# Split value-token projections, a row-paired decay and rate product, and branch gates moved into the delta rule's groups

## What is computed

```python
u = rmsnorm(h, g_mix[l])
proj = u @ w_in[l]
(rq, rk, rv, rgate, dq, dk_, dv_, dz, db, da, gate_r, gate_d) = split(proj)
ro = retention_chunkwise(rotary(rq), rotary(rk) * RET_DK ** -0.5, rv)      # 8 heads, values of 128
y_ret = (silu(rgate) * groupnorm(ro)) @ w_ret_br[l]
g = -exp(dn_a_log[l]) * softplus(da + dn_dt_bias[l])                       # summed along the tokens of a chunk
do = gated_delta_chunkwise(cq, ck, cv, g, beta)                            # 8 heads, (I + A)^-1 per chunk
y_dn = (norm(do) * silu(dz)) @ w_dn_br[l]
merged = sigmoid(gate_r) * y_ret + sigmoid(gate_d) * y_dn
h = h + merged @ w_o[l]                                                    # then a convolutional FFN
```

```python
w = -softplus(-(w0 + tanh(w_lo) @ w2)) - 0.5      # decay, w_lo is 64 wide, w2 is 64 x 2048
a = sigmoid(a0 + a_lo @ a2)                       # rate,  a_lo is 64 wide, a2 is 64 x 2048
decay = exp(-exp(w))
y = wkv7_scan(r, decay, k, v, -kk, kk * a)        # 32 heads of 64, worked two heads (a pair) at a time
```

## Time and profile before

| What | Value |
|---|---|
| Time, median of 3 runs | 1546.98 us (1546.9 to 1548.11) |
| Profiled execution's own time | 1548.26 us |
| Its span in the trace | 1546.5 us |
| PE busy | 1492.3 us, 96% |
| DVE, ACT, POOL busy | 1004.3, 861.8, 49.0 us |
| Chain that ended last | PE 88%, ACT 5%, DVE 4%, issue 2%, DMA 1% |
| HBM | 107 GB/s over the span |

### The profile page before, as it was taken

How to read it: one execution, slowest core, us unless ns; L and a number is a source line. 1 busy time by engine, 2 the same in 40 slices (tenths; PEclk the granted TensorE clock), 3 DMA queues, 4 the chain that set the end, 5 groups by cost and what they waited for, 6 DMA issues and landing times.

```text
span 1546.5 us, 27065 instructions
## 1 busy us (share of the span) xinstructions
PE 1492.3 (96%) x10620; PEld 1323.7 (86%) x10620; DVE 1004.3 (65%) x1907; ACT 861.8 (56%) x2071; POOL 49.0 (3%) x28
## 2 busy tenths in 40 slices
PE   7999999999999999898899999999999999999997
PEld 7599877877899999797788898988889887789986
DVE  3368386454768875687777777777777414666764
ACT  3256443455557775555666666666666414565653
POOL 1144100000000000000000000000000000000000
PEclk9999999999999999999999999999999999999999
DMA  9364232212445555332111101111011126333331
GB/s 376 115 226 167 93 109 82 83 55 78 141 164 191 183 172 191 109 110 82 56 56 56 56 29 56 55 56 55 30 56 56 42 96 228 113 111 130 115 124 40
DMA packets 25822, 167.81 MB, mean 109 GB/s; under 512 B 3680, under 2 KB 5088, under 8 KB 6112
## 3 DMA queue, kind: packets, MB, share of 16 engines
q1 hardware_dynamic: 24512, 164.97, 30.7%
q10 hardware_dynamic: 1184, 1.11, 0.2%
HBM read 165.03 MB, written 1.05 MB: 107 GB/s over the span
## 4 chain that ended last, share of the span: by engine, by line
PE 88%; ACT 5%; DVE 4%; issue 2%; DMA 1%; SPq 0%; DVEq 0%; ACTq 0%
PE bank L765 9%; PE bank L766 9%; PE bank L767 9%; PE bank L1108 4%; PE bank L1091 4%; PE bank L895 3%; PE bank L841 3%; PE bank L1258 3%; PE bank L1242 3%; PE bank L1121 3%; PE bank L1093 3%; PE bank L1092 3%; PE bank L749 2%; PE bank L779 2%; PE bank L1235 1%
## 5 line engine op out<-in xcount | busy, mean ns | idle before, releaser
L677 DVE TENSOR_TENSOR ring_lo<-ring,w_hi_rw 128x1024 fp32r<-128x1024 f32 x117 | 142.7, 1222 | 37.4 <-ACT w_hi_rw L1522 36.3
L1522 ACT ACTIVATE w_hi_rw<-ring 128x1024 fp32r<-128x1024 f32 x117 | 122.7, 1051 | 52.1 <-PE bank L767 31.0
L677 DVE TENSOR_TENSOR w_lo<-ring,w_hi 128x1024 fp32r<-128x1024 f32 x80 | 98.5, 1233 | 75.8 <-ACT w_hi L1522 74.8
L1091 PE MATMUL bank<-x_hi,w_hi_rw 128*128 128x272 f32 x384 | 135.2, 352 | 0.1
L1490 ACT ACTIVATE arena<-bank 128x272 f32<-128x272 f32 (+2 forms) x165 | 66.7, 406 | 112.0 <-PE bank L767 47.4
L1522 ACT ACTIVATE w_hi<-ring 128x1024 fp32r<-128x1024 f32 x98 | 103.3, 1057 | 20.8 <-PE bank L767 15.0
L1093 PE MATMUL bank<-x_hi,ring_lo 128*128 128x272 f32 x384 | 110.9, 289 | 0.0
L1092 PE MATMUL bank<-x_lo,w_hi_rw 128*128 128x272 f32 x384 | 110.8, 289 | 0.0
L765 PE MATMUL bank<-u_hi,w_hi 128*128 128x256 f32 x320 | 91.0, 284 | 1.4 <-DVE w_lo L677 1.4
L767 PE MATMUL bank<-u_hi,w_lo 128*128 128x256 f32 x320 | 90.7, 284 | 0.0
L766 PE MATMUL bank<-u_lo,w_hi 128*128 128x256 f32 x320 | 90.7, 283 | 0.0
(11 more groups left out here) (506 smaller groups left out, 4446.0 us busy)
## 6 DMA issues: line engine op xcount, KB each, us to landing
ring<-wstream SPq DMA_DIRECT2D x151, 1024.0 KB, 4.9
con<-consts SPq DMA_DIRECT2D x1, 2400.0 KB, 15.2
h<-xT SPq DMA_DIRECT2D x1, 1024.0 KB, 6.2
arena<-wlora ACTq DMA_DIRECT2D x1, 1024.0 KB, 4.7
out<-arena SPq DMA_DIRECT2D x4, 256.0 KB, 2.6
arena<-decays SPq DMA_DIRECT2D x2, 384.0 KB, 5.7
gain_post<-gains SPq DMA_DIRECT2D x1, 512.0 KB, 5.9
arena<-decays SPq DMA_DIRECT2D x1, 256.0 KB, 6.2
```

The lines of the kernel that those rows point to most:

```text
L677: ops.tensor_tensor(lo, whole, hi.bitcast(F32), ALU.subtract).then_inc(S(signal), 1)
L1091: nc.tensor.matmul(b[:, 0:T2], w_hi, x_hi[:, x, k, :], start=k == 0, stop=False)
L1522: nc.scalar.activation(hi, whole, ACT.Copy).then_inc(S("w_hi_ready"), 1)
```

## The change

- **Value tokens split.** `project_tokens` uses the split form. Its 64 blocks become eight more units (`unit_start` now runs over them), each rounded by ACT and lowered by DVE or POOL. Per unit it works on both token halves in two banks, which are both done at the end of the call. `ahead` in the splitting loops shifts by eight units.
- **Row sums in portions.** `rows_decay` becomes `rows_step` after head 3 and `rows_sum` after head 4.
- **Decay and rate side by side.** `lo` is one array; the decay product reads partitions 0 to 63 of `wl` and `lo`, the rate product 64 to 127. Every pair now has the order decay, rate, key, query, norm sum, value, bonus, and a slot `low_rank` between the Gram matrices of chunks 1 and 2 holds the first two. The zeroing of `lo` on POOL goes.
- **Gates in parts.** ACT makes the sigmoids in eight parts of 512 columns, at levels 2 to 5 of groups 1 (`gr`) and 2 (`gd`), and at level 6 of the same groups an exp of a single column. DVE splits its weight unit and multiplies `gr` with `u` ahead of the last group's normalising.

```diff
-R_K, R_W, R_A, R_R, R_KK, R_V, R_BONUS = range(7)
-RW_OUTS = (8, 1, 1, 8, 1, 8, 1)
+R_W, R_A, R_K, R_R, R_KK, R_V, R_BONUS = range(7)
+RW_OUTS = (1, 1, 8, 8, 1, 8, 1)
-FILL = {"start": 1, "bonus": 1, "grams": 5, "gram0": 4, "first": 3}
+FILL = {"start": 1, "bonus": 1, "low_rank": 2, "grams": 3, "gram0": 5, "first": 2}
...
-        lo = area(taken[0], 2, T2)
+        lo = area(taken[0], T2)
...
-        unit_start = list(range(4 * DT, 64, UB)) + list(range(128, 384, UB))
+        unit_start = list(range(4 * DT, 384, UB))
...
-            def project_tokens(lhs, kt, spans):
-                b0 = blk[0]
-                for t, (a, n) in enumerate(spans):
-                    blk[0] = b0
-                    b = free_bank()
-                    for k in range(kt):
-                        ins = nc.tensor.matmul(b[0:n, :], lhs(k)[:, a:a + n], weights(4), start=k == 0, stop=k == kt - 1)
-                    ins.then_inc(S("proj_done"), 1)
+            def project_tokens(x_hi, x_lo):
+                banks = []
+                for n in range(DT // 2):
+                    i = unit_at[blk[0]]
+                    blk[0] += UB
+                    pe.wait_ge(S(("w_lo_even", "w_lo_odd")[i % 2]), i // 2 + 1)
+                    for t in range(2):
+                        if n == 0:
+                            banks.append(free_bank())
+                        b, tokens = banks[t], slice(t * P, (t + 1) * P)
+                        for k in (2 * n, 2 * n + 1):
+                            w_hi, w_lo = [w[:, k % 2 * 512:k % 2 * 512 + 512] for w in unit(i)[1:3]]
+                            nc.tensor.matmul(b[:, :], x_hi[:, k, tokens], w_hi, start=k == 0, stop=False)
+                            nc.tensor.matmul(b[:, :], x_lo[:, k, tokens], w_hi, start=False, stop=False)
+                            ins = nc.tensor.matmul(b[:, :], x_hi[:, k, tokens], w_lo, start=False, stop=k == DT - 1)
+                        if n == DT // 2 - 1:
+                            ins.then_inc(S("proj_done"), 1)
+                        elif t == 1:
+                            ins.then_inc(S("unit_used"), 1)
...
-                        ins = nc.tensor.matmul(b[:, 0:T2], wl[:, q * P:(q + 1) * P], lo[:, j - R_W, :], start=True, stop=True)
+                        r = slice(64 * (j - R_W), 64 * (j - R_W) + 64)
+                        ins = nc.tensor.matmul(b[:, 0:T2], wl[r, q * P:(q + 1) * P], lo[r, :], start=True, stop=True)
...
                 grams(p, 1)
+                fill(fill_end(p, "low_rank"))
                 grams(p, 2)
...
             for g in range(2):
+                split_hi(4 + 4 * g + 3 + HALVES)
                 for t in range(2):
                     take(vtok[:, t, g * 512:(g + 1) * 512], n=512)
-                if g == 0:
-                    split_hi(4 + HALVES)
...
+                    if g in (1, 2) and 2 <= l <= 5:
+                        part_ = (gr, gd)[g - 1][:, 2 * l - 4:2 * l - 2, :]
+                        nc.scalar.activation(part_, part_, ACT.Sigmoid).then_inc(S("gates_ready"), 1)
+                    elif g in (1, 2) and l == LEVELS - 1:
+                        nc.scalar.activation(eps_col(3), eps_col(0), ACT.Exp)
...
-            nc.scalar.activation(gr, gr, ACT.Sigmoid)
-            nc.scalar.activation(gd, gd, ACT.Sigmoid).then_inc(S("gates_ready"), 1)
...
+            split_even(4 + 4 + 3)
             dve.wait_ge(S("swapped"), 1)
...
                 if hd == 3:
-                    rows_decay()
+                    rows_step()
+                elif hd == 4:
+                    rows_sum()
...
+            split_both(first_units + 3)
+            dve.wait_ge(S("gates_ready"), 8)
+            dve.wait_ge(S("proj_taken"), 68 + 7)
+            V_.tensor_tensor(gr[:, 0:7, :], gr[:, 0:7, :], u[:, 0:7, 0:T1], ALU.mult)
+            dve.wait_ge(S("proj_taken"), 68 + 8)
+            V_.tensor_tensor(gr[:, 7, :], gr[:, 7, :], u[:, 7, 0:T1], ALU.mult)
             for quarter in range(4):
                 dn_inverse(3, quarter)
             for i in range(2):
                 dn_scale(3, i)
             dn_gate(3)
-            split_both(first_units + 3)
             lower_dn(3)
-            dve.wait_ge(S("gates_ready"), 1)
-            V_.tensor_tensor(gr, gr, u[:, :, 0:T1], ALU.mult)
-            dve.wait_ge(S("proj_taken"), 68 + 8)
```

More of the change, by code:

```diff
@@ L163, in outs_at @@
     q, r = divmod(n, sum(RW_OUTS))
-    sizes = [RW_OUTS[j] for j in rw_order(q)]
-    return len(RW_OUTS) * q + sum(1 for i in range(len(sizes)) if sum(sizes[:i + 1]) <= r)
-def rw_order(q):
-    return (R_W, R_A, R_K, R_R, R_KK, R_V, R_BONUS) if q == 0 else range(len(RW_OUTS))
+    return len(RW_OUTS) * q + sum(1 for i in range(len(RW_OUTS)) if sum(RW_OUTS[:i + 1]) <= r)
 def rw_at(q, j):
-    return len(RW_OUTS) * q + list(rw_order(q)).index(j)
+    return len(RW_OUTS) * q + j
 CONV_FROM = (8, 0, 16)
@@ L473, in build @@
         wl = area(taken[0], INNER)
-        lo = area(taken[0], 2, T2)
-        assert taken[0] == XG_LO
+        lo = area(taken[0], T2)
+        assert taken[0] <= XG_LO
         cs, dd, Wc, kk2, sdk, kp = [area(XG_LO + i * T2, T2) for i in range(6)]
@@ L1065, in fill @@
                     q, k = divmod(filled[0], sum(RW_OUTS))
-                    for j in rw_order(q):
+                    for j in range(len(RW_OUTS)):
                         if k < RW_OUTS[j]:
@@ L1860, in _ @@
                     taken_n[0] += 1
-                    act.wait_ge(S("lo_zeroed"), 2)
-                    nc.scalar.activation(lo[0:64, 0, :], bank[i % 2][0:64, 0:T2], ACT.Tanh)
-                    nc.scalar.activation(lo[64:128, 1, :], bank[i % 2][64:128, 0:T2], ACT.Copy).then_inc(S("proj_taken"), 1)
+                    nc.scalar.activation(lo[0:64, :], bank[i % 2][0:64, 0:T2], ACT.Tanh)
+                    nc.scalar.activation(lo[64:128, :], bank[i % 2][64:128, 0:T2], ACT.Copy).then_inc(S("proj_taken"), 1)
                     round_x(4)
@@ L1991, in _ @@
                 tanh_table()
+                take_until(fill_end(p, "low_rank"))
                 split_rw(p + 1, R_V)
@@ L2288, in _ @@
             for s, first in enumerate(CONV_FROM):
-                ahead = 4 + 8 * (s + 1) + 2
+                ahead = 12 + 8 * (s + 1) + 2
                 split_even(ahead)
@@ L3014, in gemm_sizes @@
     for p in range(PAIRS):
-        n += [DT if RW_OUTS[j] > 1 else 0 for j in rw_order(p)]
+        n += [DT if n_ > 1 else 0 for n_ in RW_OUTS]
     n += [len(m) * (k1 - k0) for m, k0, k1 in OUT_PIECES] + [2 * DT - 1, 1] + [DT] * 5 + [0, 0, 8] * 4
```

27 lines of the change are left out of this document (10 added, 17 removed).

## The result

The changed kernel took 1536.42 us (median of 4 runs, 1533.75 to 1537.93); the kernel before, run beside it, 1547.55 us. The ratio is 0.9926, with a 95% interval of 0.9909 to 0.9943: 11.5 us less, give or take 2.7. Forecast were 16.4 us less and a time of 1530.6.

The account below looks back on a forecast made before the run. PE was taken to bound the kernel almost everywhere. Terms of -5.1, -0.5, -2.9 and -7.9 us, row sums 0, sum to -16.4, giving a median of 1530.6 us from 1546.98; range 1526 to 1537.5, held at 0.8.

Parts of the forecast that it names:

- Value tokens, forecast -5.6: Value-token calls: split matmuls save 5.1 us of PE time, and the wait ahead of the first call closes, 0.5 us.
- Row sums, forecast 0: Head 5 of the retention stage: PE's wait ends with the decay tables' transfer, not the row sums, so worth 0.
- Gates, forecast -2.9: Delta-rule groups and what follows: -2.4 us from PE's wait, -1.5 from full clock, +1.0 from sigmoids in groups 1 and 2.
- The gap: PE's wait before the split y_dn outputs after group 3: moving DVE's product earlier gains 2.4 us, bounds 1.9 and 2.6.
- level 5: Groups 1 and 2: ACT has no gap there, so the sigmoid part costs 0.5 us each, +1.0 us in all.
- the clock: Behind the y_dn gap: with the long PE idle gone, full clock was expected, gaining 1.5 us, bounds 0 and 1.7.
- rival (e): Near the gates: no PE wait closes, ACT's rounding being late, and the clock still falls; 3.9 us less gain, 1534.5; chance 0.06.
- Decay and rate, forecast -7.9: RWKV pairs: the two products overlap on partition halves, saving 0.5 us a pair, 7.5 for 15, plus 0.4 for pair 0.
- Rival (a): RWKV pairs: decay and rate do not overlap, saving only 0.2 us a pair; 5.5 us less gain, 1536; chance 0.12.
- (b): Value-token stage starves: DVE and POOL collide and PE waits for units; 3 us less gain, 1533.6; chance 0.15.
- Rival (c): RWKV pairs: ACT becomes the bound, the saving turns into waits, only other parts gain, 8.5 us; 1538.5; chance 0.06.
- (d): RWKV pairs: late bonus sum delays the tanh table load and PE's key; 18 us slower, 1565; chance 0.03.

Follow-up runs that it names:

- the last experiment: Changed kernel with the late square, the last sigmoid part at level 6 and the decay tables issued earlier, together: 1527.02 us, ratio 0.9864 to the kernel before.
- the gates alone: Kernel before with only ACT's sigmoid parts and DVE's weight unit and gate product ahead of the normalising: 1547.11 us, ratio 0.9995.
- the part at level 6: Changed kernel with the last sigmoid part of groups 1 and 2 at level 6 instead of 5: 1533.04 us, ratio 0.9908 to the kernel before.
- the early tables: Changed kernel with the last three decay tables' transfer issued behind weight chunk 29 instead of 30: 1533.27 us, ratio 0.9909 to the kernel before.

## Why the prediction was right, and where it fell short

**Value tokens, forecast -5.6.** Right: 6.3 us gained, 0.4 given back. A record of the split form takes 10.91 / 48 = 0.227 us, close to the 0.233 read from the earlier trace rows; the wait ahead of the first call was worth the full 0.5. Not counted was the entry into the split form: before, the first convolution record was followed only after 0.52 us instead of 0.12, behind plain matmuls, and that 0.4 is gone. The rotary step's matmuls between the calls take 3.26 us instead of 3.45, which makes the rest. The rival of a starved stage was real in its mechanism and harmless. The rotary step's product ran beside POOL's unit and took 3.63 us instead of 2.29:

```profile
57.97 3.63 DVE L2275 TENSOR_TENSOR sq<-sq,arena 128x2048 f32<-128x2048 f32 x1
61.52 1.21 DVE L672 TENSOR_TENSOR w_lo<-ring,w_hi 128x1024 fp32r<-128x1024 f32 x1
```

```profile
57.05 2.40 POOL L672 TENSOR_TENSOR w_lo<-ring,w_hi 128x1024 fp32r<-128x1024 f32 x1 [6.52 <-ACT w_hi L1531]
```

DVE's instruction had both inputs in SBUF and ended 2.15 us after POOL's, about its own length: it waited for POOL's to end. That fits the Trainium skill, "SBUF — State Buffer", section "SBUF: two separate sides". The unit was done at 62.73, 1.0 us ahead of PE's need: of the 2.6 us of margin 1.6 were eaten, 1.3 of them by this collision.

**Row sums, forecast 0.** Right. That the transfer bounds head 5 was read rightly, and so was that it would come along when PE gets there sooner, but not quite: the wait grew from 1.32 to 1.74 us.

**Gates, forecast -2.9.** The gap (-2.4; measured -2.54) and level 5 (+1.0; +1.05) were right to 0.15 us. The step that failed is the clock: -1.5 us was taken as the consequence of one gap, from one profile, with 0 as a bound and next to no chance given to it (0.06, in rival (e)). Four other executions with the same gap had full clock behind it. What the trace of before showed there was a draw; on average the term was near 0, 0.3 us by 1 in 5 (an estimate from five profiles).

**Decay and rate, forecast -7.9.** The mechanism was right: the halves run at the same time, 0.46 us for both, even below the 0.51 of the estimate. The Trainium skill's rule in "TensorE: Matmul & The Clock Gate", section "Part 3: Packing small matmuls — row/col tiling", gave 0.45 and is the better number. The step that was off is what comes back as a wait: 0.1 to 0.15 us a pair were put down for ACT's copy, 0.28 it is. I had ACT done 0.15 us behind PE's arrival. Counted from the start of the Gram matrices, PE was there 0.03 us earlier than reckoned, the copy ended 0.05 later, and PE went on 0.05 after its end. What I had not asked is why the copy stood there: behind the square, which nobody awaits at that point. Measured are 0.38 us a pair, 5.7 for the 15, which is inside the bounds of 0.35 to 0.65 and at their lower end. For pair 0, 0.1 instead of 0.4: from its first record to the first key output it is 690.88 - 689.45 = 1.43 us, since ACT must first empty the banks that the rate product and the key need (its copies start at 689.55 and 690.29). The reading of the earlier trace rows, that a lone product on 64 partitions costs no less than one on 128, was too mild: by the starts it costs 0.1 us more. For the change itself that did not matter.

**The sum.** Forecast -16.4. Of it the pairs took 2.1 us, the clock 1.5 or a little less, and the feed-forward stage 0.2, where the timelines differ by how the slow stretches lie over the gap there; the tokens gave 0.25 more and the gates' other terms 0.1. That is the 12.9 of the table. The runs say 11.5 and 12.8. Neither reaches the forecast of 16.4; the time fell into the range because the range reached up to where the rivals lay, not because the sum was right. Rival (a) fell with the pair's trace (0.46 us for both products), (b) with the unit that was 1.0 us early, (e) with the gap that closed. Rival (c) was right in kind: ACT became the bound of a pair, but it took only 0.28 of the 0.66 us that PE saved there (0.38 + 0.28), not all. (d) needed more than 1.1 us of new wait a pair.

## What to carry to other kernels

- Ask of an engine that is off the critical path what stands in its row between the event that releases it and the result that is awaited, and whether all of it must stand there. One ACT instruction of 0.43 us moved by four places was worth 4.7 us here, nearly as much as the whole edit that had made it critical.
- Matmuls on halves of the partitions paid here only side by side with their other half; apart they were a loss of 0.2 us each. They stood between work of the same shape, and a pair of halves among matmuls on 128 partitions was not tried. Each of the two edits alone cost 5 to 6 us, though for the new place most of that was a wait for another engine: look which engine a loss belongs to before you call the edit bad.
- Don't book a clock change from one profile. Look for the same gap in further executions first.

## What was not expected of the hardware

- Where matmuls of 64 rows and matmuls of 128 rows follow each other, some 0.1 us each way is lost: 0.3 us for the four records on 128 between the Gram matrices, 0.2 us for a lone product on 64 (0.65 against 0.46), 0.1 us on two records in the retention stage (0.53 against 0.43). That the change of rows is the cause is inferred from these three places.
- A slow stretch of 3.4 us costs 1.7 us when PE works through it, and nothing when it lies ahead of a wait of that size that another engine ends. In the last experiment it lay from 248 to 252 us; the wait behind it shrank from 2.2 to 0.54 us, and the stage was not longer. Three more runs (the gates alone, the part at level 6, the early tables) show the same, with waits of 0.53 to 0.55 us; in three with the long stretch the wait is gone and 0.9 us is lost.

```profile
252.93 0.66 PE L941 MATMUL bank<-con,arena 128*128 128x128 f32 x4 [0.54 <-DVE arena L2409]
```

- The first split record behind plain float32 ones is followed later than the others: 0.52 us instead of 0.12 at the first convolution output of before, behind 512-column matmuls, and 0.42 instead of 0.23 at 52.66 in the changed kernel, behind 256-column ones.
